# A two-layer trunk whose down projection forms seven pairs of row blocks, not five, in half-block products

## What is computed

```python
x = x + rms_norm(mix, post_mix_g[l])
h = rms_norm(x, pre_ffn_g[l])
gu = jnp.einsum('bsd,df->bsf', h, w_gate_up[l])
gate, up = gu[..., :FFN_HIDDEN], gu[..., FFN_HIDDEN:]
y = jnp.einsum('bsf,fd->bsd', jax.nn.silu(gate) * up, w_down[l])
x = x + rms_norm(y, post_ffn_g[l])
```

## Time and profile before

| | |
|---|---|
| median of 3 runs | 1073.05 us (1073.04 to 1073.09) |
| profiled execution | 1073.02 us |
| its span in the profile | 1071.2 us |
| PE busy | 1062.2 us, 99% of the span |
| DVE, ACT, POOL busy | 743.7, 622.0, 527.5 us |
| granted clock of PE | 1.0 of full |

### The profile page before, as it was taken

One profiled execution on the slowest core, in us unless ns is written; L12 is line 12 of the kernel. 1 busy time (PEld: TensorE's weight loads), 2 busy tenths in 40 slices (PEclk: granted clock), 3 DMA queues, 4 the chain that ended last, 5 costly groups with the idle time before them and its releaser, 6 DMA issues.

```text
span 1071.2 us, 17731 instructions
## 1 busy us (share of the span) xinstructions
PE 1062.2 (99%) x6728; PEld 953.9 (89%) x6728; DVE 743.7 (69%) x1207; ACT 622.0 (58%) x1223; POOL 527.5 (49%) x402
## 2 busy tenths in 40 slices
PE   9999999999999999999999999999999999999997
PEld 7888888999999999888878888889999999998886
DVE  4376644878888886876554756548888888868764
ACT  6767784756556554344457578757555555643441
POOL 4535264457666664223444344634666666632250
PEclk9999999999999999999999999999999999999999
DMA  8423213424334333565353222133333433427442
GB/s 295 148 59 99 76 46 97 157 79 120 99 100 119 96 103 119 196 207 186 98 154 114 79 79 80 59 107 110 111 110 97 119 101 98 119 88 258 142 152 78
DMA packets 149496, 127.24 MB, mean 119 GB/s; under 512 B 4122, under 2 KB 120356, under 8 KB 149412
## 3 DMA queue, kind: packets, MB, share of 16 engines
q1 hardware_dynamic: 149396, 126.11, 37.8%
q10 hardware_dynamic: 16, 0.00, 0.0%
HBM read 119.80 MB, written 6.29 MB: 118 GB/s over the span
## 4 chain that ended last, share of the span: by engine, by line
PE 97%; DVE 1%; ACT 1%; DMA 1%; issue 0%; SPq 0%; DVEq 0%; ACTq 0%
PE banks L686 30%; PE banks L688 30%; PE banks L687 30%; PE banks L751 2%; PE banks L779 2%; PE banks L695 1%; PE banks L764 1%; PE banks L1002 1%; PE banks L790 1%; DMA x_rows<-in_x_dram 1%; PE banks L797 0%; ACT junk L1222 0%; DVE x_rows L1753 0%; ACT junk L1269 0%; DVE banks L1742 0%
## 5 line engine op out<-in xcount | busy, mean ns | idle before, releaser
L624 POOL TENSOR_TENSOR w_lo<-raw,w_hi 128x512 fp32r<-128x512 f32 x164 | 222.7, 1384 | 340.7 <-ACT w_hi L1214 340.7
L642 POOL TENSOR_TENSOR w_lo<-raw,w_hi 128x512 fp32r<-128x512 f32 x200 | 261.7, 1319 | 145.7 <-ACT w_hi L1295 141.3
L686 PE MATMUL banks<-xg_hi,w_hi 128*128 128x256 f32 (+1 forms) x880 | 273.5, 311 | 0.0
L688 PE MATMUL banks<-xg_lo,w_hi 128*128 128x256 f32 (+1 forms) x880 | 271.3, 308 | 0.0
L687 PE MATMUL banks<-xg_hi,w_lo 128*128 128x256 f32 (+1 forms) x880 | 271.2, 308 | 0.0
L1295 ACT ACTIVATE w_hi<-raw 128x512 fp32r<-128x512 f32 x200 | 124.8, 631 | 115.3 <-DVE raw L2007 61.3
L688 PEld LDWEIGHTS banks<-xg_lo,w_hi 128*128 128x128 f32 x880 | 168.1, 191 | 8.5
L686 PEld LDWEIGHTS banks<-xg_hi,w_hi 128*128 128x128 f32 x880 | 168.1, 191 | 8.3
L687 PEld LDWEIGHTS banks<-xg_hi,w_lo 128*128 128x128 f32 x880 | 168.1, 191 | 7.5
L686 PE MATMUL banks<-s_part,w_hi 128*128 128x256 f32 x480 | 135.8, 283 | 0.0
L687 PE MATMUL banks<-s_part,w_lo 128*128 128x256 f32 x480 | 135.8, 283 | 0.0
(11 more groups left out here) (219 smaller groups left out, 2053.5 us busy)
## 6 DMA issues: line engine op xcount, KB each, us to landing
raw<-in_w_gate_up_dram SPq DMA_DIRECT2D x88, 512.0 KB, 4.2
raw<-in_w_down_dram SPq DMA_DIRECT2D x54, 512.0 KB, 4.3
raw<-in_w_in_dram SPq DMA_DIRECT2D x40, 512.0 KB, 3.8
raw<-in_w_out_dram SPq DMA_DIRECT2D x16, 512.0 KB, 3.4
x_spill<-x_rows SPq DMA_DIRECT2D x8, 512.0 KB, 4.9
x_rows<-x_spill SPq DMA_DIRECT2D x8, 512.0 KB, 6.3
raw<-in_w_down_dram SPq DMA_DIRECT2D x10, 256.0 KB, 2.6
x_rows<-in_x_dram SPq DMA_DIRECT2D x4, 512.0 KB, 7.6
```

The source lines that it names most:

```text
L624: last = tt(lo[:, piece], raw_half(l, c, h)[:, piece], hi[:, piece].bitcast(F32), ALU.subtract)
L642: tt(lo, full, hi.bitcast(F32), ALU.subtract).then_inc(w_ready, 1)
L686: mm(o, stat[0], mov[0], start=first, stop=False)
L688: return mm(o, stat[0], mov[1], start=False, stop=last)
```

## The change

Blocks 10 to 13 move from plain chunks to pairs 5 and 6. `NP` goes from 5 to 7, L10 and R10 are gone from the list, and one L chunk (L14) stands before the pairs, none between them. The fourth activation sum (S4) is now made in place in `hid_full`, in two parts: pairs 0 to 3 (`EARLY`), then pairs 4 to 6 (`LATE`). Q products go in another order (T1, T2, B22). ACT copies product five out of its banks (`keep_p5`), DVE adds it to product six and gathers the two in eight additions for the right and left halves together, not ten. The first two rows of the left half are squared and multiplied by their gain earlier, during the Q chunks.

```diff
@@ -40,17 +40,18 @@
 
     C_VG, C_QK, C_VA, C_QK2, C_U, C_OUT, C_GU = 0, 2, 4, 6, 8, 10, 14
     C_DOWN = C_GU + FT
-    NP = 5
+    NP = 7
     K0_PLAIN = 2 * NP
-    DOWN = [("L", 10), ("P", 0), ("P", 1), ("L", 14), ("P", 2), ("P", 3), ("P", 4), ("L", 18),
-            ("Q", 0), ("Q", 1), ("Q", 2), ("Q", 3), ("Q", 4), ("R", 10), ("R", 14), ("R", 18)]
+    DOWN = [("L", 14)] + [("P", p) for p in range(NP)] + [("L", 18)] + [("Q", p) for p in range(NP)] + \
+        [("R", 14), ("R", 18)]
     NC = C_DOWN + len(DOWN)
     CE = 1024
     LAST = NC - 1
     C_P, C_Q = [[C_DOWN + DOWN.index((kind, p)) for p in range(NP)] for kind in "PQ"]
-    C_L_END, C_R0 = C_DOWN + DOWN.index(("L", 18)), C_DOWN + DOWN.index(("R", 10))
+    C_L_END = C_DOWN + DOWN.index(("L", 18))
+    EARLY, LATE = (0, 4), (4, NP)
     P_B11, P_B21, P_T3, P_T4 = range(4)
-    Q_B22, Q_T1, Q_T2 = range(3)
+    Q_T1, Q_T2, Q_B22 = range(3)
 
 
...
@@ -195,14 +196,20 @@
                    "A22": (hid_hi[:, second_of_pair, right], hid_lo[:, second_of_pair, right]),
                    "S3": (part_hi[:, 0:NP, :], hid_lo[:, first_of_pair, right]),
                    "S1": (part_hi[:, NP:2 * NP, :], hid_hi[:, first_of_pair, right]),
-                   "S2": (part_hi[:, 2 * NP:3 * NP, :], part_lo[:, 0:NP, :]),
-                   "S4": (part_lo[:, NP:2 * NP, :], part_lo[:, 2 * NP:3 * NP, :])}
+                   "S2": (part_lo[:, 0:NP, :], part_lo[:, NP:2 * NP, :]),
+                   "S4": (hid_lo[:, second_of_pair, left], hid_hi[:, second_of_pair, left])}
         H_FULL = {"S3": hid_full[:, 1, first_of_pair, right], "S1": hid_full[:, 0, first_of_pair, right],
-                  "S2": part_full[:, 1, 0:NP, :], "S4": part_full[:, 1, 2 * NP:3 * NP, :]}
-        H_SUMS = ("S3", "S1", "S2", "S4")
+                  "S2": part_full[:, 1, NP:2 * NP, :], "S4": hid_full[:, 0, second_of_pair, left]}
+        H_HIGHS = [("S3", None), ("S1", None), ("S2", None), ("S4", EARLY), ("S4", LATE)]
+        H_LOWS = [("S3", None), ("S1", None), ("S2", EARLY), ("S4", EARLY), ("S2", LATE), ("S4", LATE)]
+
+        def pairs_of(t, pairs):
+            return t[:, slice(*pairs) if pairs else slice(0, NP), :]
+
+        p5 = part_full[:, 0, 2 * NP:2 * NP + 2, :], part_full[:, 1, 2 * NP:2 * NP + 2, :]
 
         def y_left_of(r):
-            return hid_full[:, r // 2, 4 + 2 * (r % 2):6 + 2 * (r % 2), left]
...
@@ -590,12 +598,12 @@
 
                 for c in range(C_DOWN + 2, NC):
                     load(l, c)
-                    r = c - C_P[2]
-                    if r == 0:
+                    if c == C_P[2]:
                         sp.wait_ge(w_done, upto(l, C_DOWN - 1, B22))
-                    if 0 <= r < ST:
-                        sp.dma_start(x_rows[:, r, :], x_spill[r * P:(r + 1) * P, :]).then_inc(x_back, 16)
-                    elif r == ST:
+                    for r, behind in enumerate((C_P[2], C_P[4], C_P[6], C_L_END)):
+                        if c == behind:
+                            sp.dma_start(x_rows[:, r, :], x_spill[r * P:(r + 1) * P, :]).then_inc(x_back, 16)
+                    if c == C_L_END:
                         load_gain(gpost[:, :], post_ffn_g[l], gpost_landed)
                         if l < L - 1:
                             load_gain(gpre[:, :], pre_mix_g[l + 1], gpre_landed)
...
@@ -937,7 +945,7 @@
                 pair_product(l, c, P_B21, "A12", 0, False, False)
                 pe.wait_ge(pair_ready, pair_upto(l, c, P_T3))
                 if p == 0:
-                    pe.wait_ge(h_ready, 4 * l + 1)
+                    pe.wait_ge(h_ready, 6 * l + 1)
                 pair_product(l, c, P_T3, "S3", 6, True, True)
                 pe.wait_ge(pair_ready, pair_upto(l, c, P_T4))
                 pair_product(l, c, P_T4, "A22", 2, False, False)
@@ -945,19 +953,21 @@
             def right_pair(l, p):
 
                 c = C_Q[p]
+                pe.wait_ge(pair_ready, pair_upto(l, c, Q_T1))
+                if p == 0:
+                    pe.wait_ge(h_ready, 6 * l + 4)
+                    pe.wait_ge(p7_added, 2 * (l + 1))
+                elif p == LATE[0]:
+                    pe.wait_ge(h_ready, 6 * (l + 1))
+                pair_product(l, c, Q_T1, "S1", 6, True, True)
+                pe.wait_ge(pair_ready, pair_upto(l, c, Q_T2))
+                if p < 2:
+                    pe.wait_ge(y_left_added, 4 * l + 2 * (p + 1))
+                pair_product(l, c, Q_T2, "S2", 0, True, True)
                 pe.wait_ge(pair_ready, pair_upto(l, c, Q_B22))
                 if p == 0:
-                    pe.wait_ge(h_ready, 4 * (l + 1))
                     pe.wait_ge(p1_kept, 2 * (l + 1))
                 pair_product(l, c, Q_B22, "S4", 4, True, False)
-                pe.wait_ge(pair_ready, pair_upto(l, c, Q_T1))
-                if p == 0:
-                    pe.wait_ge(p7_added, 2 * (l + 1))
-                pair_product(l, c, Q_T1, "S1", 6, True, True)
-                pe.wait_ge(pair_ready, pair_upto(l, c, Q_T2))
-                if p == 0:
-                    pe.wait_ge(y_left_added, 4 * l + 2)
-                pair_product(l, c, Q_T2, "S2", 0, True, True)
 
             def down_rows(l, r, between=lambda: None):
 
...
@@ -1655,22 +1671,31 @@
                 silu_11(FT - 1)
                 silu_21(FT - 1)
                 hidden_high(FT - 1)
-                h_high("S3")
+                h_high(0)
                 for c in range(C_DOWN + 1, NC):
                     if paired(c):
                         for i in range(DONE_OF[kind_of(c)]):
                             pair_high(c, i)
                     else:
                         both_high(l, c)
-                    if c == C_P[NP - 1]:
-                        for name in H_SUMS[1:]:
-                            h_high(name)
+                    if c == C_P[2]:
+                        h_high(1)
+                        h_high(2)
+                    elif c == C_P[6]:
+                        h_high(3)
                     elif c == C_L_END:
                         keep_p1(0)
                         keep_p1(1)
+                    elif c == C_Q[2]:
+                        h_high(4)
+                    elif c == C_Q[3]:
+                        square_a(2 * l + 1, l, 0)
+                        square_a(2 * l + 1, l, 1)
                     elif c == LAST - 1:
-                        for r in range(ST):
-                            square_a(2 * l + 1, l, r)
+                        keep_p5(0)
+                        keep_p5(1)
+                square_a(2 * l + 1, l, 2)
+                square_a(2 * l + 1, l, 3)
                 if l < L - 1:
                     boundary(2 * l + 1, l, (l + 1, 0), (l + 1, 1))
                 else:
...
@@ -2060,22 +2087,32 @@
                             tt(a21, a21, o[:, right], ALU.add)
                         tt(hid_lo[:, f, :], o[:, :], hid_hi[:, f, :].bitcast(F32), ALU.subtract).then_inc(hid_ready, 1)
 
-                def h_low(name):
-
-                    hi, lo = H_PARTS[name]
-                    dve.wait_ge(h_hi_ready, 4 * l + H_SUMS.index(name) + 1)
-                    tt(lo, H_FULL[name], hi.bitcast(F32), ALU.subtract).then_inc(h_ready, 1)
-
-                def h_sum(step):
-
-                    a11, a12 = [[t.bitcast(F32) for t in H_PARTS[name]] for name in ("A11", "A12")]
-                    s1, s2, s4 = [H_FULL[name] for name in ("S1", "S2", "S4")]
-                    if step == 0:
-                        tt(s2, s1, a11[0], ALU.subtract).then_inc(h_added, 1)
-                    else:
-                        dve.wait_ge(h_added, 4 * l + step)
-                        one, other, op = ((s2, a11[1], ALU.subtract), (a12[0], s2, ALU.subtract), (s4, a12[1], ALU.add))[step - 1]
-                        tt(s2 if step == 1 else s4, one, other, op).then_inc(h_added, 1)
+                def h_low(n):
+
+                    name, pairs = H_LOWS[n]
+                    hi, lo = [pairs_of(t, pairs) for t in H_PARTS[name]]
+                    dve.wait_ge(h_hi_ready, 5 * l + (H_HIGHS.index((name, pairs)) if name == "S4" else H_HIGHS.index((name, None))) + 1)
+                    if name == "S2":
+                        dve.wait_ge(h_added, 6 * l + (3 if pairs == EARLY else 5))
+                    tt(lo, pairs_of(H_FULL[name], pairs), hi.bitcast(F32), ALU.subtract).then_inc(h_ready, 1)
+
+                def s2_sum(step):
+
+                    a11 = H_PARTS["A11"][step].bitcast(F32)
+                    if step == 1:
+                        dve.wait_ge(h_added, 6 * l + 1)
+                    tt(H_FULL["S2"], H_FULL["S2" if step else "S1"], a11, ALU.subtract).then_inc(h_added, 1)
+
+                def s4_sums(pairs):
+
+                    s2, s4 = pairs_of(H_FULL["S2"], pairs), pairs_of(H_FULL["S4"], pairs)
+                    a12 = [pairs_of(t, pairs).bitcast(F32) for t in H_PARTS["A12"]]
+                    n = 6 * l + (2 if pairs == EARLY else 4)
```

(89 more changed lines are left out.)

8 lines of the change are left out of this document (4 added, 4 removed).

## The result

The changed kernel takes 1087.95 us (median of 4 runs, 1086.68 to 1088.94), 14.9 us more than the 1073.05 of before. The ratio is 1.0139, with a 95% interval of 1.0121 to 1.0156. The forecast was 1084.2.

A forecast was written before the change was run, and what follows sets the result against it. PE's stream was taken as the bound. Stalls of 4.2 (P stretch) and 4.1 us (tail) in each of two layers, less 5.44 for 24 matmuls, gave 11.2 us slower, 1084.2 from 1073.05; range 1077 to 1090.

The forecast's parts named there:

- The P stretch, 4.2 us a layer: Seven P chunks: PE waits for DVE 0.4 at P1, 0.95 at P2, 0.2 at P5 and 2.65 us at P6.
- P5's 0.2: At P5: the low part is there at 463.1, PE wants it at 462.9, a wait of 0.2 us.
- P6's 2.65: At P6: the first low part comes at 471.2, PE wants it at 468.55, a wait of 2.65 us.
- The walk: Step-by-step times of DVE and PE through the P and Q chunks, a P chunk taking DVE 4.46 and PE 5.44 us.
- P6 waits for arithmetic: Argument against the rival of smaller stalls (1077.6, chance 0.2): P1, P2 and P6 wait for arithmetic, not loads.
- Before, L14 gave PE 10.88 us in the middle for no work of DVE: Short reason for the P stretch: DVE now has 40.6 us of work to P6's end, PE 38.1.
- The tail, 4.1 us a layer: Row 0 of R14/R18: POOL's fourth half ready at 523.3, wanted at 520.15, 3.15 us, plus 0.94 where DVE meets POOL.
- 0.94 was walked: Tail: two later gains on DVE fall inside POOL's work and cost 0.94 us more.
- The clock: Rival, chance 0.04: the clock halves where PE waits, one P chunk a layer costs 5.4 us more, 1095 in all.
- The row that I weighed against it: Argument against the clock rival: between 5.4 and 12 us the clock stayed at 1.00, PE busy 5.55 of 6.60.
- 5.44 for the matmuls: Gain from two pairs of blocks per layer changing form: 24 matmuls fewer at 0.2267 us each, 5.44 us.

The follow-up runs named there:

- e5: The changed kernel with the second steps of sums S2 and S4 cut to 8 columns on DVE, leaving their values incomplete: 1078.80 us.
- e4: The changed kernel with the low parts of R14's right half and R18's left half made on DVE, not POOL: 1084.22 us.
- e8: The changed kernel with the four reloads of x moved from behind P2, P4, P6 and L18 to behind Q3 to Q6: 1086.66 us.
- e2: The kernel of e1 with both plain chunks (L10, L14) ahead of the five P chunks and none between them: 1074.03 us.
- e1: The changed kernel with five pairs and the list of chunks of before, all other edits kept: 1073.91 us, 1.0008 of before.

## Why the prediction was right, and where it was off

**The bound and the mechanism.** Right: PE starved twice a layer, by DVE in the P chunks and by POOL at row 0. e5 and e4 took work from each and got 9.1 and 3.7 us back.

**The P stretch, 4.2 us a layer.** Measured 0.45 + 0.82 + 2.41 = 3.7. P5's 0.2 didn't show; P6's 2.65 was 2.41. The walk was good to 0.1 us on DVE and 0.25 on PE. One sentence of it was too strong: P6 waits for arithmetic, but 0.6 us of its wait come from P4's late data (e8).

**"Before, L14 gave PE 10.88 us in the middle for no work of DVE".** As a reason it isn't borne out: e2 moved L14 ahead of five pairs and took 0.1 us more than e1. What e1, e2 and e5 show is that the amount counts, the P chunks and sums that DVE must do between P0 and L18. Whether L14 in the middle of seven pairs would shorten the waits is untested.

**The tail, 4.1 us a layer.** Measured 4.02 and 4.23. That it agrees so closely is in part luck: POOL began late, and so did PE. POOL's run started at 515.41, not 513.2. R14's load waits for Q5's low parts, and these ended at 510.5, not 508.3; the 4.9 us from there to POOL's start are as walked. The whole stretch was late by then: Q0 started at 489.26, not 487.5, by the clock's 1.6 us above all, and Q4's data came at 502.54, not 500.8.

```profile
508.46 2.02 DVE L2140 TENSOR_TENSOR w_lo<-raw,w_hi 128x512 fp32r<-128x512 f32 x3
514.27 1.06 ACT L1222 ACTIVATE w_hi<-raw 128x1024 fp32r<-128x1024 f32 x1 [0.58 <-DMA raw<-in_w_down_dram]
```

PE ended Q6 at 517.83, not 516.05, so it was late by 1.8 and POOL by 2.2. Where DVE and POOL met, POOL lost about what was walked (10.88 for 10.08, 0.80 where 0.94 was walked), DVE more: 3.44 us for two gains that take 1.29 alone, and 1.22 for the operation behind them.

**The clock: the term that the forecast left out.** It stood among the rivals with 0.04 and at 5.4 us a layer, for 24 matmuls. It came beside the forecast's waits, not in place of them, and lasted eight matmuls, 1.6 us a layer. It doesn't come in each execution in the same measure: two of the four runs have a mean clock of 0.995 (1088.94, which is the traced one, and 1088.71), two of 0.998 (1087.20 and 1086.68); of these two there is no trace, and they are faster by some 1.9 us, where two falls cost 3.2. The row that I weighed against it covers two waits of 0.6 and 0.4 us at the start of the kernel, not one of 2.4. TensorE: Matmul & The Clock Gate of the Trainium skill, section "HAM oscillation", which the prediction cited for the rival, had the direction right: in this case's trace the clock fell behind the waits of 2.41 and 2.42 us.

**The sum.** Of the profiled execution, extra in layer 0: 3.7 + 1.6 in the P chunks and 4.0 in the tail; in layer 1: 3.7 + 1.6 and 4.2; together 18.8. The 0.12 to 0.15 us behind each of the 14 waits, which the walk doesn't have, are 1.8 more. Less 5.44 for the matmuls that is 15.2 of the 15.9 by which the span grew. The last 0.7 I didn't trace. Against the forecast's 11.2, the clock is 3.2 of the difference and the starts behind waits 1.8; the P stretch took 1.0 less than walked.
